# Layer norm by token tiles, router logits ahead of it, expert panels loaded as slots fall free

## The reference

```
merged = sigmoid(gate_sb) * (o_sb @ w_branch_sb) + sigmoid(gate_hg) * (o_hg @ w_branch_hgrn)
mix    = merged @ w_out
h      = layer_norm(2**0.25 * h + mix, ln1_g, ln1_b)
logits = h @ router_w + router_b                 # 32 experts
top_vals, top_idx = top_k(logits, 4);  gates = softmax(top_vals)
# for each chosen expert e of a token
hcat = h @ w_up[e] + b_up[e]                     # 1024 x 2048
x_glu = min(hcat[:, 0::2], 7);  x_lin = clip(hcat[:, 1::2], -7, 7)
y = (x_glu * sigmoid(1.702 * x_glu) * (x_lin + 1)) @ w_down[e] + b_down[e]   # 1024 x 1024
h = layer_norm(2**0.25 * h + sum(gates * y), ln2_g, ln2_b)
```

## Time and profile before

| | |
|---|---|
| time, median of 3 runs | 1888.97 us (1888.76 to 1889.19) |
| the profiled execution | 1890.32 us, of which 1889.1 us is the span of the profile |
| busy share of the span | TensorE 92%, VectorE 41%, ScalarE 31%, GpSimd 2% |
| DMA | 537.07 MB, mean 284 GB/s |
| the stretches | mixer until 883.7 us, router 883.7 to 925.5, experts to 1871.6, tail to 1889.1 |

### The profile page before, as it was taken

One profiled execution on the slowest core, in us unless ns is written; L12 is line 12 of the kernel. 1 busy time (PEld: TensorE's weight loads), 2 busy tenths in 40 slices (PEclk: granted clock), 3 DMA queues, 4 the chain that ended last, 5 costly groups with the idle time before them and its releaser, 6 DMA issues.

```text
span 1889.1 us, 24194 instructions
## 1 busy us (share of the span) xinstructions
PE 1745.8 (92%) x9215; PEld 1044.7 (55%) x9216; DVE 776.9 (41%) x1109; ACT 579.8 (31%) x754; POOL 32.1 (2%) x58
## 2 busy tenths in 40 slices
PE   7999999988999999985899999999999998999996
PEld 6779997777999898874433333333233232333332
DVE  3544456654444557865323223222232222322224
ACT  1535555543555456542111111111111111111111
POOL 0000000000000210000000000000000000000000
PEclk9999999999999999998799999999999999999998
DMA  7355554412455543312999999999999996999995
GB/s 257 134 178 178 186 200 152 177 45 82 176 188 178 182 138 133 134 45 66 398 408 428 429 428 428 428 428 428 428 428 429 428 423 268 393 428 428 429 428 225
DMA packets 84962, 537.07 MB, mean 284 GB/s; under 512 B 8736, under 2 KB 8840, under 8 KB 60328
## 3 DMA queue, kind: packets, MB, share of 16 engines
q1 hardware_dynamic: 79088, 531.64, 69.8%
q10 hardware_dynamic: 5816, 4.59, 0.8%
HBM read 535.17 MB, written 1.05 MB: 284 GB/s over the span
## 4 chain that ended last, share of the span: by engine, by line
PE 63%; DMA 26%; DVE 6%; ACT 3%; issue 2%; ACTq 0%; SPq 0%; PEldq 0%; POOL 0%; DVEq 0%; POOLq 0%
DMA expert_ring<-in_expert_w_up 25%; PE psA L1901 19%; PE psA L535 12%; PE psB L495 11%; PE psB L518 3%; PE psB L387 3%; PE psA L518 2%; PE psB L506 2%; PE psA L410 1%; DVE w_low L476 1%; PE psA L1907 1%; PE psB L342 1%; PE psB L1930 1%; PE psB L1337 1%; PE psA L982 1%
## 5 line engine op out<-in xcount | busy, mean ns | idle before, releaser
L1901 PE MATMUL psA<-expert_ring,gathered_T 128*64 128x512 f32 x1024 | 455.0, 596 | 31.6 <-DMA expert_ring<-in_expert_w_up 31.6
L1902 PE MATMUL psA<-expert_ring,gathered_T 128*64 128x512 f32 x1024 | 455.0, 596 | 0.0
L476 DVE TENSOR_TENSOR w_low<-panel_ring,w_high 128x1024 fp32r<-128x1024 f32 x220 | 267.4, 1223 | 205.8 <-ACT w_high L469 205.2
L1901 PEld LDWEIGHTS psA<-expert_ring,gathered_T 128*64 128x64 f32 x1024 | 134.8, 137 | 344.7 <-issue 280.2
L469 ACT ACTIVATE w_high<-panel_ring 128x1024 fp32r<-128x1024 f32 x220 | 230.4, 1056 | 276.6 <-PE psA L535 112.9
L1901 PE MATMUL psA<-expert_ring,activated_T 128*64 128x512 f32 x528 | 240.5, 598 | 3.2 <-ACT activated_T L2162 0.9
L1902 PE MATMUL psA<-expert_ring,activated_T 128*64 128x512 f32 x528 | 240.5, 598 | 0.0
L2292 DVE TENSOR_SCALAR normed<-psA 128x512 f32<-128x512 f32 x32 | 22.1, 691 | 393.4 <-PE psA L1902 393.4
L495 PE MATMUL psB<-hT_high,w_high 128*128 128x256 f32 x592 | 167.8, 283 | 0.0
L495 PE MATMUL psB<-hT_low,w_high 128*128 128x256 f32 x592 | 167.5, 283 | 0.0
L495 PE MATMUL psB<-hT_high,w_low 128*128 128x256 f32 x592 | 167.5, 283 | 0.0
(11 more groups left out here) (432 smaller groups left out, 2572.5 us busy)
## 6 DMA issues: line engine op xcount, KB each, us to landing
expert_ring<-in_expert_w_up SPq DMA_DIRECT2D x128, 2048.0 KB, 25.4
expert_ring<-in_expert_w_down SPq DMA_DIRECT2D x64, 2048.0 KB, 22.3
panel_ring<-in_mlp_w SPq DMA_DIRECT2D x32, 2048.0 KB, 7.8
panel_ring<-in_w_in SPq DMA_DIRECT2D x11, 2048.0 KB, 8.3
panel_ring<-in_fox_w_in SPq DMA_DIRECT2D x6, 2048.0 KB, 8.3
panel_ring<-in_lru_w_in SPq DMA_DIRECT2D x4, 2048.0 KB, 18.2
panel_ring<-in_lru_w_out SPq DMA_DIRECT2D x2, 2048.0 KB, 7.8
panel_ring<-in_fox_w_out SPq DMA_DIRECT2D x2, 2048.0 KB, 8.4
```

The source lines that it names most:

```text
L476: V.tensor_tensor(w[1], view, w[0].bitcast(F32), ALU.subtract).then_inc(s.w_low, 1)
L1901: M.matmul(ps[0:SLOTS], lhsT, rhs[0], **flags)
L1902: return M.matmul(ps[SLOTS:P], lhsT, rhs[1], **flags)
```

## The change

- The first layer norm goes tile by tile. TensorE transposes x before it is normalized; the router's weights are multiplied by the norm's gain, and the logits are put right afterwards with the row's mean, its deviation and two sums over the router's weights (`router_sums_dve`, `router_sums_pe`, `route`). The two normalizing passes (`finish_dve`) come behind the choice of experts. The last layer norm goes by tiles too.
- The small loads are issued in the mixer (`moe_loads_act`), 14 in place of 9: gain and bias of the norm also as columns, and the down biases in four pieces of 32 rows, so that the bias products take four 32-row matmuls.
- In the mixer, the transposes of `o_hg` go before the last part of panel 11, and the copies and gate multiplications are reordered. The update of tile 0 and its transposes lie inside panel 14.
- SyncE loads the first panels of expert 0 as each slot falls free. Both down panels have two slots now and the up panels one.

The core of the diff:

```diff
@@ hybrid_pe
     for i in range(4):
         product_out(k, HYBRID + 11, i, row(i), i == 0, i == 3)
-    M.wait_ge(s.hg_normed, 1)
-    transpose_pe(k, h.o_hg, 0, 4, k.psB[0], k.ident[:])
+        if i == 2:
+            M.wait_ge(s.hg_normed, 1)
+            transpose_pe(k, h.o_hg, 0, 4, k.psB[0], k.ident[:])
...
-        (1, 2): lambda: merged_T(0)})
+        (1, 1): lambda: merged_T(0)})
...
-    product_out_tiles(k, HYBRID + 14, lambda i: row(4 + i), False, True, {})
+    product_out_tiles(k, HYBRID + 14, lambda i: row(4 + i), False, True, {
+        (0, 1): lambda: router_sums_pe(k, m),
+        (1, 1): lambda: router_T_pe(k, 0)})
@@ hybrid_act
     gate_sigmoid(0)
-    highs(49, 51)
+    branch_high(1, 8)
+    highs(49, 52)
     gate_sigmoid(1)
-    branch_high(1, 8)
-    highs(51, 53)
+    moe_loads_act(k, m)
+    highs(52, 53)
     merged_high(0)
-    highs(53, 55)
+    highs(53, 56)
     merged_high(1)
-    highs(55, 60)
+    highs(56, 60)
@@ hybrid_dve
-    lows(48, 51)
+    lows(48, 49)
+    branch_low(1)
...
-    V.wait_ge(s.gate_sig, 2)
-    for tt in range(TT):
-        V.tensor_tensor(gate(0, tt), gate(0, tt), psum(tt), ALU.mult).then_inc(s.branch_read, 1)
-    branch_low(1)
+    V.wait_ge(s.gate_sig, 1)
+    V.tensor_tensor(gate(0, 0), gate(0, 0), psum(0), ALU.mult).then_inc(s.branch_read, 1)
+    lows(49, 51)
+    V.tensor_tensor(gate(0, 1), gate(0, 1), psum(1), ALU.mult).then_inc(s.branch_read, 1)
     lows(51, 52)
...
     merged_low(1)
-    lows(55, 60)
+    router_sums_dve(k, m)
+    lows(56, 60)
@@ the slots
-EXPERT_SLOTS = ((1, 2, 3, 4, 5, 6), (7, 0, 3, 4, 5, 6))
+EXPERT_SLOTS = ((1, 2, 3, 7, 0, 4), (1, 2, 3, 7, 5, 6))
+TWICE = (4, 5)
@@ moe_sp
-        n = e * 6 + (j - 5 if j >= 2 else j - 11)
+        n = e * 6 + (j - 5 if j not in TWICE else j - 11)
...
-    S.wait_ge(s.late, LATE_MOE)
-    for j in range(6):
-        if j < 3:
-            S.wait_ge(*slot_free(k, PANELS - 4 + j))
-        else:
-            S.wait_ge(s.x_updated, 10)
+    for j in range(3):
+        S.wait_ge(*slot_free(k, HYBRID + 11 + j))
         load(0, 0, j)
-    for j in range(6):
-        if j == 1:
-            S.wait_ge(*slot_free(k, PANELS - 1))
-        elif j >= 2:
-            expert_slot_free(1, j)
+    S.wait_ge(s.nat_T, 10)
+    load(0, 0, 3)
+    S.wait_ge(*slot_free(k, HYBRID + 14))
+    load(0, 0, 4)
+    S.wait_ge(*hybrid_done(s, 14))
+    load(0, 0, 5)
+    for j in TWICE:
+        load(1, 1, j)
+    for j in range(4):
+        expert_slot_free(1, j)
         load(1, 1, j)
@@ new functions
+def moe_loads_act(k, m):
+    nc, A, s, a = k.nc, k.nc.scalar, k.s, k.a
+    for i, name in enumerate(("ln1_g_2", "ln1_b_2")):
+        A.dma_start(m.ln1[:, i, :], a[name][0].partition_broadcast(P)).then_inc(s.late, 16)
+        with nc.allow_non_contiguous_dma(reason="one value per partition"):
+            A.dma_start(m.ln_cols[:, i, :], a[name][0].rearrange("(c p) -> p c", p=P)).then_inc(s.late, 16)
+    A.dma_start(m.rw[:], a["router_w_2"][0].rearrange("(k p) n -> p k n", p=P)).then_inc(s.late, 16)
+    A.dma_start(m.rb[:], a["router_b_2"][0].partition_broadcast(P)).then_inc(s.late, 16)
...
+def router_sums_dve(k, m):
+    V, s, dve = k.nc.vector, k.s, k.dve
+    V.wait_ge(s.late, LATE_MOE)
+    weights = lambda i: m.ln_cols[:, i, :].unsqueeze(2).to_broadcast([P, KD, NE])
+    V.tensor_tensor(m.rw_b[:], m.rw[:], weights(1), ALU.mult).then_inc(*dve.step())
+    V.tensor_tensor(m.rw[:], m.rw[:], weights(0), ALU.mult).then_inc(*dve.step())
+    V.wait_ge(*dve.last())
+    for i, w in enumerate((m.rw, m.rw_b)):
+        V.tensor_reduce(m.sums[:, i, :], w[:].rearrange("p c n -> p n c"), axis=AX.X, op=ALU.add).then_inc(s.router_sums, 1)
@@ moe_dve
+    update(0)
+    deviation_dve(k, m, 0, 0)
+    update(1)
+    route(0)
+    deviation_dve(k, m, 0, 1)
+    route(1)
     for tt in range(TT):
+        finish_dve(k, m, 0, tt, k.x)
@@ the bias products
-    for tt, ps in enumerate((m.S, k.psA[:, 2:4, :])):
-        for half in range(2):
-            last = M.matmul(ps[:, half, :], m.gT[:, tt * P:(tt + 1) * P], m.bdown[:, half * 512:(half + 1) * 512],
-                            start=True, stop=True)
+    for c in range(4):
+        tt, half, rows = c // 2, c % 2, slice(NE * c, NE * (c + 1))
+        to = (m.S, k.psA[:, 2:4, :])[tt]
+        last = M.matmul(to[:, half, :], m.gT[rows, tt * P:(tt + 1) * P], m.bdown[rows, :], start=True, stop=True)
```

247 lines of the change are left out of this document (134 added, 113 removed).

## The result

The changed kernel takes 1861.9 us (median of 4 runs, 1860.12 to 1863.03) where the kernel before takes 1889.08 (1888.76 to 1890.75) in the same session: ratio 0.9854, 95% interval 0.9836 to 0.9871, 27.2 us less. The forecast was 1857.6, 31.4 us less, with a range of 1850 to 1865. The profiled execution has a span of 1861.8 us, so 27.3 less than the span of before, 1889.1.

A forecast was written before the change was run, and what follows sets the result against it. It took the kernel to be bound by the stream of 192 expert panels at about 428 GB/s, tied to expert 0's start. 9.9 + 22.1 - 0.2 - 0.4 = 31.4 us gained, so 1857.6 us, range 1850 to 1865.

The forecast's parts named there:

- Part A: Mixer's tail: reordering shortens TensorE's waits and removes slow matmuls, gain 9.9 us (bounds 3 to 11).
- 14 loads at 0.49 each, 6.9 us, costed at nothing: Mixer's tail: ScalarE's issues of the small loads take 6.9 us but fall where it would wait for TensorE anyway.
- rival 1: Mixer's tail stays bare through late small loads or ScalarE's 14 issues: gain there only 3, time 1864.5; chance 0.12.
- Part B: From the mixer's end to expert 0's start: 41.8 us shrinks to 19.75, gain 22.1.
- in quarters of 32 rows they look like L1907, whose eight records take 1.09: Gather to expert 0: the down bias products, now 3.6 us, would take 1.09, leaving 6.9 of 9.5.
- rival 2: TensorE stays fast through counting and gather, since its gaps are shorter: 3 us less, at least 1853; chance 0.11.
- Part C: Expert panel stream: 1.1 us better after the start, 1.3 worse around long expert 21, 0.2 loss in all.
- rival 3: Long expert 21 costs more, nothing of expert 22 loadable ahead: hole 11 instead of 6.6, time 1862; chance 0.08.
- the use of 27.2 us for expert 0: Panel stream: expert 1's first panel is used 27.2 + 4.5 us after expert 0's start, and (2,0) waits for that.
- Part D: Kernel's tail: last norm by tiles fills a 1.07 us wait but repeats small operations, 0.4 us loss.
- Rival 4: Panel stream: one slot per up panel starves it in every expert; slower than now beyond 1.0 us each; chance 0.04.
- Rival 5: No change in time: the stream's end stays put because earlier loads only fill eight slots; chance 0.02.

The follow-up runs named there:

- e1: Changed kernel with the expert slots of the kernel before put back: 1860.94 us.
- e5: Changed kernel without the second pass for an expert with more than 64 tokens (expert 21's tokens behind the 64th left out): 1837.93 us.
- e6: As e5, but with the eight slots used as one ring in panel order and the loop written out over four experts: 1829.98 us.
- e12: As e2, but experts 2 to 7 load their two down panels ahead of their four up panels: 1849.18 us.
- e9: Changed kernel with expert 0's loads begun only when the mixer's products and the update of x are done: 1868.9 us.
- e10: Changed kernel with the eight expert bias loads moved from the mixer's tail to behind the update of tile 0 of x: 1864.53 us.
- e4: Changed kernel with the old order in the mixer's tail, keeping the small loads, router sums, layer norm and slots of the change: 1878.48 us.
- e7: Kernel before with only the new order in the mixer's tail: 1881.38 us.
- e2: Changed kernel with 16 products that nobody reads put into TensorE's idle gaps: 1857.41 us.
- e3: Changed kernel with the eight slots as one ring in panel order and the loop written out over four experts, second pass kept: 1910.14 us.
- e8: Changed kernel with both the unread products of e2 and the old slots of e1: 1858.16 us.
- e11: As e3, but with TensorE's code shortened, the rest of an expert's first pass standing once instead of twice: 1920.66 us.

## Why the prediction was right, and where it was off

**What bounds the kernel.** Right: DMA moves 428 GB/s in the steady windows in every kernel here that does not wait for instructions, and times follow the stream's holes (e1, e5, e6 and e12 to 1 us; e9 missed its forecast, and its holes counted afterwards give 5 of 7 us).

**Part A** (9.9 forecast, 10.1 measured). The waits were forecast as 1.3, 0.5, 0.6 and 0.7 to 0.9; the trace has 1.36, none, 0.25 (ahead of tile 1's merged transposes, 852.35) and 0.67, so the first and fourth came as worked out and the middle two all but vanish. The step "14 loads at 0.49 each, 6.9 us, costed at nothing" had the wrong size and the right price: ScalarE was busy with them from 833.74 to 844.1, 10.4 us, as router_w and router_b take 1.73 and 2.35 us to issue instead of 0.46 and 0.60. e10 shows that the tail does not pay for the eight bias loads among them, so rival 1 did not come; e4 shows that it pays (3.2 us) in the old order. The addition of parts is also not what it seems: the order alone gains 7.2 (e7), its removal loses 16.6 (e4).

**Part B** (22.1 forecast, 20.5 measured). Right: VectorE's chain from the mixer's end to the last choice takes 8.95 us (9.1 forecast), counting and gather are at the low clock. The step that failed is "in quarters of 32 rows they look like L1907, whose eight records take 1.09": that row was at the full clock. Here the bias products take 2.0 instead of 1.09 and the rows' transposes 1.13 instead of 0.74. The gather began where it was forecast (886.42, worked out as 886.6), and from it to expert 0 it took 8.5 us instead of 6.9: this is the whole 1.6, because the clock came back after expert 0's first products (898.57) and not by the rows' transposes, as before. I took the low clock for counting and gather and let it end there; no row said when it ends. e2 removes it and gains 4.5 us, which is rival 2's mechanism bought with products. e7 shows the same delay in the kernel before. In e5's profile the same code had its full clock at the rows' transposes (0.74 us), so the moment differs between executions too. That the rest of part B came as forecast is read from the trace; no run takes it apart.

**Part C** (0.2 loss forecast, 2.8 measured). From expert 21's start to the last product it is 1843.8 - 1498.65 = 345.2 us, 344.1 before: 1.1 worse, forecast 1.3. (22,0) and (23,0) are asked for 25.3 and 71.8 us after that start, worked out as 24.7 and 71.3. So rival 3 did not come, and e5 finds 24.0 us for the long expert where the holes were worked out as 23.6. What failed is the use of 27.2 us for expert 0: it took 30.6 (894.89 to 925.50), 1.8 more for the low clock in the up bias and the first panel, and 1.85 more for the issue wait (0.2 of it in place of another wait). As (2,0) waits for expert 1's first panel, the whole stream came as much later. The instruction wait had no place in the sum; it is the term that was missing. In expert 0 no row of before shows it, but the trace of before has its larger kin, 4.08 us at 1592.05, and that one is in the forecast unseen, as the hole of 17 us was worked out from rows behind it.

**Part D** (0.4 loss forecast, 0.5 measured).

**Rival 4** (one slot per up panel starves the stream) is excluded: e1 has the old slots and the same time, and no steady window of 20 us is under 424 GB/s. **Rival 5** (earlier loads only fill slots) is excluded by e9: their early start is worth 7 us. The Trainium skill (DMA: Bandwidth & Descriptors, "Rules for kernel authors"), the page that spoke against the change, has one descriptor per element where the last dimension is not contiguous, so 1,024 for each of the two column loads. The page of the profile has 10,864 packets under 512 B, 2,128 more than before, which agrees with 2 x 1,024, and what they seem to cost is the slow issue of router_w and router_b behind them (argued from the order of the queue, not tried alone).

**Open.** No run takes part B apart, the largest of the four. e7, which has of the change only the mixer's order, is 19.5 us slower than the changed kernel; e9 finds 7.0 of that in the early loads and e1 nothing in the slots. How the rest is divided between the norm by tiles and the small loads (VectorE waited 3.17 us for router_b before, at 891.98) was not tried. What decides about the issue wait of the first experts is not settled either. All its long gaps (1.7 to 2.5 us, in the changed kernel, e2, e3, e4, e8, e9, e10 and e12) lie where the stream is full (420 GB/s or more in the window of 10 us), and where it was empty within the 5 us ahead the gap is short or absent (0.4 in e1; none in expert 0 of before, e7 and e8). But expert 1 of before has a full stream (426 GB/s or more) and no gap either. Between bodies of 1,270 and 2,080 instructions nothing was run, so whether the ring would gain with all of the computation and a shorter loop is not known.

## What to carry to other kernels

Find the transfer stream's holes and count the panels left behind the last one; their sum gave the totals of e1, e5, e6 and e12 within 1 us, and it says which reordering pays (e12: 8 us for a few lines in the issue order). When a row at the full clock is used for a step behind a stretch with gaps, price it at both levels of the clock, up to the first long run of products. Before a loop is unrolled further, count the instructions of its body: the ring was worth 7.9 us without the second pass, and with it the longer loop made the kernel 48 slower.

## What was not expected of the hardware

- A loop of four experts with all of its code waits about 2.0 us at a jump and 3.9 us where it starts again (e3), or 1.2 to 1.4 at an expert's start and 7.3 to 7.8 where it starts again (e11), and moves 133 or 117 packets of instructions instead of 44; with 1,270 or fewer TensorE instructions in the body there is none of it in the steady state. A rare second pass costs such a wait too: 4.08 us at the expert behind it, in every kernel here of the short loop that has the pass.
- The clock came back at different places behind the same gather: at the transposes of the gathered rows in the kernel before and in e5's profile, but 8.5 us behind the gather's end in the changed kernel (890.1 to 898.57). Products in the gaps kept it from falling at all (e2).
- In the changed kernel and e4, ScalarE's issue of a small load took 0.34 to 0.60 us, but 1.73 to 2.53 us for the two behind the loads of separate 4-byte values.
